# Expert weights exchanged in half slots of 1 MB, with a wait for each half on both sides, and down products in row order

## The reference, cut to what matters

```python
def hier_moe(h, w_router_group, w_router_expert, w_exp_gate, w_exp_up, w_exp_down):
    ...
    out = jnp.zeros((B * T, D), jnp.float32)
    for grp in range(N_GROUPS):
        wgt = comb * (g_sel == grp)[:, None]
        hg = jnp.einsum('nd,edf->enf', hf, w_exp_gate[grp])
        hu = jnp.einsum('nd,edf->enf', hf, w_exp_up[grp])
        hid = jax.nn.silu(hg) * hu * wgt.T[:, :, None]
        out = out + jnp.einsum('enf,efd->nd', hid, w_exp_down[grp])
    return out.reshape(B, T, D)
```

## Time and profile before

| | |
|---|---|
| median of the runs | 1875.35 us (1875.28 to 1878.07, 3 runs) |
| the profiled execution, its own time | 1873.54 us |
| its span, first to last instruction | 1871.8 us |
| mean granted clock of PE | 0.972 of full speed |
| PE busy | 1751.0 us, 94% |
| bytes read from memory | 618.65 MB, 336 GB/s over the span |
| expert loads | 64 of gate, 64 of up, 64 of down, 2048 KB each |

### The profile page before, as it was taken

How to read it: one execution, slowest core, us unless ns; L and a number is a source line. 1 busy time by engine, 2 the same in 40 slices (tenths; PEclk the granted TensorE clock), 3 DMA queues, 4 the chain that set the end, 5 groups by cost and what they waited for, 6 DMA issues and landing times.

```text
span 1871.8 us, 32911 instructions
## 1 busy us (share of the span) xinstructions
PE 1751.0 (94%) x14031; PEld 1106.9 (59%) x14031; DVE 665.4 (36%) x1444; ACT 470.1 (25%) x778; POOL 211.8 (11%) x295
## 2 busy tenths in 40 slices
PE   5689999999989999899899999999999999999997
PEld 2268779988856666799644444445444454444544
DVE  1145554464673544643322222222221222222224
ACT  3044333344531211344411111111111111111114
POOL 1000000011028880343000000000000000000000
PEclk9889999999999999899999999999999999999998
DMA  9989885585388779341799999999999999999993
GB/s 365 419 285 336 295 326 144 188 263 158 131 313 332 302 307 376 100 162 46 320 420 430 428 429 427 430 427 430 427 430 427 430 427 430 427 430 427 430 427 155
DMA packets 124944, 629.64 MB, mean 336 GB/s; under 512 B 10469, under 2 KB 78493, under 8 KB 83360
## 3 DMA queue, kind: packets, MB, share of 16 engines
q1 hardware_dynamic: 118974, 608.45, 80.9%
q0 software_dynamic: 5120, 17.44, 2.7%
q10 hardware_dynamic: 754, 2.33, 0.3%
HBM read 618.65 MB, written 9.56 MB: 336 GB/s over the span
## 4 chain that ended last, share of the span: by engine, by line
PE 42%; DMA 13%; DVE 1%; issue 1%; SPq 0%; ACT 0%; POOL 0%; DVEq 0%; POOLq 0%; ACTq 0%
PE pb L2681 24%; DMA ring<-in_w_exp_gate 13%; PE pb L2655 4%; PE pb L2661 2%; PE pb L2689 2%; PE pb L2032 2%; PE pb L2033 2%; PE pb L2034 1%; PE pb L2662 1%; PE pb L2570 0%; DVE xt L1830 0%; SPq L502 0%; PE pb L2731 0%; PE pb L2577 0%; PE pb L2728 0%
## 5 line engine op out<-in xcount | busy, mean ns | idle before, releaser
L2681 PE MATMUL pb<-ring,pj 128*64 128x512 f32 x2048 | 460.0, 602 | 23.9 <-DMA ring<-in_w_exp_gate 23.0
L2681 PEld LDWEIGHTS pb<-ring,pj 128*64 128x64 f32 x2048 | 149.2, 138 | 298.8 <-issue 294.7
L2032 PE MATMUL pb<-ht_parts,ring_parts 128*128 128x264 f32 x1056 | 309.5, 293 | 7.3 <-DVE ring_parts L1304 6.2
L2033 PE MATMUL pb<-ring_parts 128*128 128x264 f32 x1056 | 302.1, 286 | 0.0
L2034 PE MATMUL pb<-ring_parts 128*128 128x264 f32 x1056 | 301.8, 286 | 0.0
L2689 PE MATMUL pb<-ring,pj 128*64 128x512 f32 x1024 | 223.3, 594 | 0.0
L2032 PEld LDWEIGHTS pb<-ht_parts,ring_parts 128*128 128x128 f32 x1056 | 202.0, 191 | 24.3 <-issue 16.0
L2033 PEld LDWEIGHTS pb<-ring_parts 128*128 128x128 f32 x1056 | 202.0, 191 | 0.0
L2034 PEld LDWEIGHTS pb<-ring_parts 128*128 128x128 f32 x1056 | 200.9, 190 | 0.0
L1304 DVE TENSOR_TENSOR ring_parts<-ring,ring_parts 128x2048 fp32r<-128x2048 f32 x50 | 114.6, 2292 | 173.9 <-ACT ring_parts L789 173.8
L2689 PEld LDWEIGHTS pb<-ring,pj 128*64 128x64 f32 x1024 | 72.2, 137 | 138.9 <-issue 136.9
(11 more groups left out here) (474 smaller groups left out, 1959.2 us busy)
## 6 DMA issues: line engine op xcount, KB each, us to landing
ring<-in_w_exp_gate SPq DMA_DIRECT2D x64, 2048.0 KB, 15.2
ring<-in_w_exp_up SPq DMA_DIRECT2D x64, 2048.0 KB, 17.2
ring<-in_w_exp_down SPq DMA_DIRECT2D x64, 2048.0 KB, 15.7
ring<-in_w_ada SPq DMA_DIRECT2D x32, 2048.0 KB, 14.8
ring<-in_w_in SPq DMA_DIRECT2D x24, 2048.0 KB, 9.4
pj<-in_w_ada SPq DMA_DIRECT2D x32, 1024.0 KB, 7.8
ring<-in_w_ada_final SPq DMA_DIRECT2D x16, 2048.0 KB, 13.0
ring<-in_w_out SPq DMA_DIRECT2D x8, 2048.0 KB, 8.6
```

The source lines that it names most:

```text
L2032: pe.matmul(out, hi[:, k, :], ht_lo[:, k, :], start=(k == 0), stop=False)
L2033: pe.matmul(out, lo[:, k, :], ht_hi[:, k, :], start=False, stop=False)
L2681: last = pe.matmul(pb[step // 2][SLOT * q:SLOT * q + SLOT, :], xg[:, k, SLOT * q:SLOT * q + SLOT], w[q][:, j, :], start=(k == 0), stop=(k ...
```

## The change

A slot is treated as two halves of 1 MB. `half_slot(s, part)` is a half of its columns, `half_full(s, part)` the semaphore that tells of its landing: `m_full{s}a` or `m_full{s}b`, or, for the first halves of slots 0 to 3, the slot's older semaphore `ring_full{s}` with its count at that point.

SyncE issues four loads of 1 MB for a step instead of two of 2 MB: both experts' first halves, then both experts' second halves. A partition now receives 8 KB by a load. The first halves wait for `m_half`, a new semaphore that PE increments in the middle of each step, the second ones for `m_step` as before.

PE waits for the first halves, does half of the step's products, increments `m_half`, waits for the second halves, does the rest and increments `m_step`. In the down steps a half is one row of hidden values (`c`), so the products now go over all four banks for one row and then over all four for the next. A bank is finished, and announced, in the second half of step 5.

To have room for the new semaphores others are joined: `m_wt` and `m_hp` to `m_turn`, `m_sg`, `m_wte` and `m_ht` to `m_act`, `m_ws` and `m_hid` to `m_dve`, `sv_store` and `sv_in` to `sv_moved`, with the counts adjusted. The instructions on ACT, DVE and GpSimd and their order stay.

```diff
@@ slots
+        def half_slot(s, part):
+            return ring[:, s * RING + part * (RING // 2):s * RING + (part + 1) * (RING // 2)]
+
+        def half_full(s, part):
+
+            if part == 0 and s < MIX_SLOTS:
+                return S(f"ring_full{s}"), out_loads(4 + OUT_SLOTS.index(s))
+            return S(f"m_full{s}{'ab'[part]}"), 0
@@ SyncE
-                for q in range(2):
-                    s = moe_slot(step, q)
-                    if freed is not None:
-                        sp.wait_ge(S("m_step"), freed)
...
-                    sp.dma_start(slot(s).rearrange("p (k f) -> p k f", f=src.shape[2]), src)\
-                        .then_inc(S(f"m_full{s}"), 16)
+                for part in range(2):
+                    for q in range(2):
+                        s = moe_slot(step, q)
+                        if freed is not None:
+                            sp.wait_ge(S(("m_half", "m_step")[part]), freed)
...
+                        w, n = (w_exp_gate, w_exp_up, w_exp_down)[step // 2], 4 if step < 4 else 1
+                        at = (step % 2 * 2 + part) * n
+                        src = w[0].rearrange("g e a b -> (g e) a b")[bass.ds(pair * 2 + q, 1)]
+                        src = src.rearrange("o (p k) f -> p (o k) f", p=P)[:, at:at + n, :]
+                        sp.dma_start(half_slot(s, part).rearrange("p (k f) -> p k f", f=src.shape[2]), src)\
+                            .then_inc(half_full(s, part)[0], 16)
@@ PE
-                for q in range(2):
-                    s = moe_slot(step, q)
-                    pe.wait_ge(S(f"m_full{s}"), (t * 2 + step // 3 + 1) * 16)
...
-                    for n in range(4):
-                        for j in range(2):
-                            c = (step - 4) * 2 + j
-                            for q in range(2):
-                                last = pe.matmul(pb[2 + n][SLOT * q:SLOT * q + SLOT, :], hid_t[:, c, SLOT * q:SLOT * q + SLOT],
-                                                 w[q][:, j, n * BANK:(n + 1) * BANK], start=(c == 0), stop=(c == 3))
-                        if step == 5 and n < 3:
-                            last.then_inc(S("m_yb"), 1)
-                last.then_inc(S("m_step"), 1)
+                for part in range(2):
+                    for q in range(2):
+                        full, before = half_full(moe_slot(step, q), part)
+                        pe.wait_ge(full, (t * 2 + step // 3 + 1) * 16 + before)
+                    w = [half_slot(moe_slot(step, q), part) for q in range(2)]
+                    if step < 4:
+                        for j in range(4):
+                            k = step % 2 * 8 + part * 4 + j
...
+                    else:
+                        c = (step - 4) * 2 + part
+                        for n in range(4):
...
+                            if c == 3 and n < 3:
+                                last.then_inc(S("m_yb"), 1)
+                    last.then_inc(S(("m_half", "m_step")[part]), 1)
```

More of the change, by code:

```diff
@@ L486, in expert_load @@
             def expert_load(pair, step, freed=None):
-                for q in range(2):
-                    s = moe_slot(step, q)
-                    if freed is not None:
-                        sp.wait_ge(S("m_step"), freed)
[L492 to L501, removed]
-                    sp.dma_start(slot(s).rearrange("p (k f) -> p k f", f=src.shape[2]), src)\
-                        .then_inc(S(f"m_full{s}"), 16)
+                for part in range(2):
[3 more added lines that the diff above has]
+                            sp.wait_ge(S(("m_half", "m_step")[part]), freed)
+                        elif s < MIX_SLOTS:
+                            sp.wait_ge(S("out_ps"), 8 + 2 * OUT_SLOTS.index(s) + 2)
+                        else:
+                            sp.wait_ge(S("out_ps"), KD)
+                        w, n = (w_exp_gate, w_exp_up, w_exp_down)[step // 2], 4 if step < 4 else 1
[4 more added lines that the diff above has]
+                            .then_inc(half_full(s, part)[0], 16)
             for step in range(3):
@@ L1181, in moe_act @@
                     act.wait_ge(S("m_step"), t * STEPS + 2)
-                    act.activation(sg, pb[0][:], ACT.Silu).then_inc(S("m_sg"), 1)
-                    act.wait_ge(S("m_wt"), t + 1)
-                    act.copy(pwt[:, 0:NP_], pb[7][:, 0:NP_]).then_inc(S("m_wte"), 1)
+                    act.activation(sg, pb[0][:], ACT.Silu).then_inc(S("m_act"), 1)
+                    act.wait_ge(S("m_turn"), t * 2 + 1)
+                    act.copy(pwt[:, 0:NP_], pb[7][:, 0:NP_]).then_inc(S("m_act"), 1)
                     moe_gather_out(ps * GA + i * 4 + 4, 0)
-                    act.wait_ge(S("m_hp"), t + 1)
-                    act.copy(hid_t, pb[6][:].rearrange("p (c s) -> p c s", s=P)).then_inc(S("m_ht"), 1)
+                    act.wait_ge(S("m_turn"), t * 2 + 2)
+                    act.copy(hid_t, pb[6][:].rearrange("p (c s) -> p c s", s=P)).then_inc(S("m_act"), 1)
                     for n in range(4):
@@ L1856, in moe_dve @@
                         last = dve.tensor_copy(w_slot[r, :], pb[6][r, q:q + 1])
-                    last.then_inc(S("m_ws"), 1)
+                    last.then_inc(S("m_dve"), 1)
                     moe_dispatch(ps * 17 + i + 1, i + 1)
-                    dve.wait_ge(S("m_ws"), t + 1)
-                    dve.wait_ge(S("m_sg"), t + 1)
+                    dve.wait_ge(S("m_dve"), t * 2 + 1)
+                    dve.wait_ge(S("m_act"), t * 3 + 1)
                     dve.wait_ge(S("m_step"), t * STEPS + 4)
                     dve.scalar_tensor_tensor(out=sg, in0=sg, scalar=w_slot, in1=pb[1][:], op0=ALU.mult, op1=ALU.mult)\
-                        .then_inc(S("m_hid"), 1)
+                        .then_inc(S("m_dve"), 1)
                     moe_gather_out(ps * GA + i * 4 + 4, 1)
@@ L2671, in moe_step @@
             def moe_step(t, step):
-                for q in range(2):
-                    s = moe_slot(step, q)
-                    pe.wait_ge(S(f"m_full{s}"), (t * 2 + step // 3 + 1) * 16)
[L2676 to L2679, removed]
-                        for q in range(2):
[L2681 to L2684, removed]
-                    for n in range(4):
-                        for j in range(2):
-                            c = (step - 4) * 2 + j
+                for part in range(2):
[6 more added lines that the diff above has]
+                            k = step % 2 * 8 + part * 4 + j
+                            for q in range(2):
+                                last = pe.matmul(pb[step // 2][SLOT * q:SLOT * q + SLOT, :], xg[:, k, SLOT * q:SLOT * q + SLOT],
+                                                 w[q][:, j * FF:(j + 1) * FF], start=(k == 0), stop=(k == KD - 1))
+                    else:
+                        c = (step - 4) * 2 + part
+                        for n in range(4):
@@ L2731, in moe_pe @@
                         last = pe.transpose(pb[7][:, c * P:(c + 1) * P], disp[:, c, :], ident[:])
[L2732 removed]
+                    last.then_inc(S("m_turn"), 1)
                     moe_step(t, 3)
[L2735 removed]
+                    pe.wait_ge(S("m_act"), t * 3 + 2)
                     pe.wait_ge(S("m_dp"), n + 2)
                     moe_gather(0)
[L2738 removed]
+                    pe.wait_ge(S("m_dve"), t * 2 + 2)
                     for c in range(4):
                         last = pe.transpose(pb[6][:, c * P:(c + 1) * P], sg_in_rows[:, c, :], ident[:])
[L2741 removed]
+                    last.then_inc(S("m_turn"), 1)
                     moe_gather(1)
[L2743 removed]
+                    pe.wait_ge(S("m_act"), t * 3 + 3)
                     pe.wait_ge(S("m_add"), t * KD + KD)
```

15 lines of the change are left out of this document (8 added, 7 removed).

## The result

| | before | after |
|---|---|---|
| median of the runs | 1875.35 us (1870.94 to 1880.11, 7 runs) | 1882.74 us (1878.94 to 1885.22, 7 runs) |
| ratio | | 1.0031, 95% interval 1.0017 to 1.0046 |
| span of the profiled execution | 1871.8 us | 1877.1 us |

The changed kernel is slower by 0.31%, about 6 us; the interval reaches from 3 to 9 us, and the two medians themselves lie 7.4 us apart. The forecast was 1881.3 us, and "slower by over 0.2%" with a chance of 0.60.

A forecast was written before the change was run, and what follows sets the result against it. The full DMA queue was taken as the bound. 6.3 and 4.1 us gained against 14.6 and 2.4 lost, by the stream's count +6.0 us, gave 1879.5 for the profiled execution and 1881.3 us for the median; range 1871.5 to 1889.

The forecast's parts named there:

- The queue sets the pace: Loop over expert pairs: the full DMA queue, 428.5 GB/s, sets 58.73 us a pair; PE's own work is 56.21 us.
- The price of 8 KB packets: Expert weight loads: half slots give 8 KB packets, 0.038 us more per MB on 383 MB, 14.6 us lost.
- p: Time 1 MB (1,048,576 bytes) takes in a full queue: 2.447 us before, forecast 2.485 with 8 KB packets.
- The lower bound: Full queue: 8 KB packets cost nothing extra, p = 2.447 us; as rival "faster" 1867.2 us, chance 0.08.
- the upper one: Full queue: from the time of one packet, 8 KB costs 2.2% more for a byte, p = 2.501 us.
- The small-price rival: Full queue: 8 KB packets only 0.5 to 1.3% dearer, p 2.459 to 2.479, 1871.6 to 1879.1 us; chance 0.32.
- The rival with a cost for each load: Expert loads: each pays something queued 2 MB loads hide; at 0.05 us each, +19 us over no price; chance 0.05.
- The sum: Expert stream: start 896.8 plus 383 x 2.485 gives 1848.6, plus 3.6 of products 1852.2 us, +6.0 against before.
- The tail: End of the loop: PE work behind the last byte falls from 7.7 us to 3.6, 4.1 us gained.
- second way of counting: Whole change: 6.3 and 4.1 us gained, 14.6 and 2.4 lost; said to differ from the sum by 0.8 us.
- The dry queue: Loop start, 915 to 945 us: 6.3 us without data, all to go through the earlier release of first halves.
- The clock risk: PE in the last pair: granted clock falls after some 2.3 us waits, costing up to 1.6 us; within the forecast case.

The follow-up runs named there:

- p4_gateup: Kernel before with gate and up loads of 2 MB in four 4 KB runs per partition, down loads untouched: ratio to before 1.0136, +27.0 us to the last product.
- p8_whole: Kernel before with each 2 MB load in two separate 8 KB runs per partition, whole-slot exchange kept: ratio to before 1.0080, +13.7 us to the last product.
- late_release: Changed kernel with both halves requested only when the whole earlier step is through: ratio to before 1.0037, 961.9 us from burst to last product.
- late_start: Changed kernel with PE waiting for both halves before a step's first product, release still by halves: ratio to before 1.0056, 964.0 us to last product.
- row_order: Kernel before with only the down products reordered, row by row over the four banks: ratio to before 1.0006, 952.7 us to last product.
- mixed: Kernel before with halves only in steps 3 to 5 of the first pair, the second and the last pair: 1869.48 us median, ratio to before 0.9967.
- mixed_start: The mixed kernel with halves at the start alone, last pair exchanged whole: 951.8 us from burst to last product, -1.2 against before, one run.

## Why the prediction was right

*The queue sets the pace.* Right. In all kernels with a 128-partition load the pair's period follows the rate and nothing else: 58.7 us at 429 GB/s, 59.64 at 422, 60.5 at 416 (p4_gateup).

*The price of 8 KB packets.* The step on which the sign hung, and right: p = 2.485 us was taken from a stretch of w_ada loads in the earlier trace rows, and 2.485 is what the expert loads take. The lower bound (no price) and the upper one (from the records' durations, 2.501) both missed it. The records do last 315 ns for an 8 KB packet in the changed kernel too, but their sum is 101.3% of the time of 16 engines, so neighbouring ones overlap by about 4 ns, as the choice assumed. The small-price rival, for which the three cycles of the Trainium skill spoke, fell with p8_whole and p4_gateup: about 9 ns a packet. The rival with a cost for each load fell with p8_whole.

*The sum.* From the burst to the last landing it gave 1848.6 - 893.2 = 955.4 us, measured 955.6 and 955.7; to the last product 959.0, measured 959.4 and 959.5; against before +6.0, measured +6.4 and +6.5. The tail was to be 3.6 us and is 3.8. One slip in the forecast changes nothing in this: its second way of counting (14.6 + 2.4 - 6.3 - 4.1) gives +6.6, so the two ways differ by 0.6 us, not 0.8.

*The parts.* The dry queue: gone, as said. But its worth was put at 6.3 us of the sum, and late_release shows 2.4. These are different comparisons. By the count of the queue from burst to last landing, with 3.6 us of start-up, 7.0 us are without data before (945.4 - 3.6 - 382 x 2.447), 2.7 in late_release and 0.2 in the change (955.6 - 3.6 - 383 x 2.485). So most of the dry time is already gone in late_release, where the first burst is 1 MB longer and the packets smaller, and only the rest hangs on `m_half`; the forecast had counted the 2.4 us of that longer burst as a loss of its own. The tail: 4.1 us forecast, 3.9 measured from the last landing; late_start loses 4.5 in all, 1.7 of them by the clock. Row order at nothing: right, by row_order. Joined semaphores and SyncE's issues at nothing have no run of their own; what the sum leaves over is 0.4 us.

*What was off.* PE waits 3.0 us in a pair where 3.4 were forecast; the full waits start at 1195 us, as forecast, with a short one of 0.4 us at 1140. The clock risk was put on the changed kernel, and it was the other way round: from 1100 to 1800 us its clock is 1.00, before 0.99. PE's clock fell after some waits of 2.2 us and more (in every kernel here with a wait for whole slots), never after the waits of 1.2 to 1.4 us of the change. In the steady part that is worth nothing, since the next wait takes it back; at the very end it is worth 1.7 us, and it cost that in late_start, mixed and mixed_start.

*The median.* 1882.74 against 1881.3. A good part of that agreement is luck: medians of the same kernel before were 1875.35, 1873.75 and 1877.28 us over three sets, a spread as large as half the effect, and the changed kernel's median lies 3.8 us above its profiled execution, the fastest of seven, where the forecast added 1.8. The ratios, 1.0031 and 1.0026, are what to go by; the forecast's was 1.0032, well inside their intervals (1.0017 to 1.0046 and 1.0011 to 1.0042).

## What to carry to other kernels

Where a queue is full, count packets before splitting loads: a release that came earlier bought nothing there (late_release: the same 422 GB/s), and each packet costs its price (about 9 ns here) in every pass. Split only where the profile shows the queue dry (the start of a stream) or an engine working behind the last byte (its end), and keep the long runs in between. To price a packet size that the kernel does not have yet at that place, look for another stretch of the same profile with that size and a full queue, and take its rate, not the mean duration of its packets.

## What the runs showed of the hardware

- Queued loads of 128 partitions: 2.447 us for 1 MB in 16 KB packets, 2.485 in 8 KB, 2.558 in 4 KB (by p4_gateup); about 9 ns for each packet on each of the 16 engines. In 8 KB packets loads of 1 MB and of 2 MB ran at the same rate (295.38 and 295.36 MB in 700 us).
- The same bytes in loads of 64 neighbouring partitions move at 216 GB/s instead of 429, and in loads of 32, alternating between the two halves of the partitions, at 250, with all engines busy. This had not been expected at all. A load for half of the partitions was the most expensive split of all that were tried; why, no run shows.
- PE's granted clock went to the lower of its two levels for a part of the next step after some waits of 2.2 to 3.2 us (step 0 then takes 8.78 us in most cases, instead of 7.09), not after others of the same length, and never after waits of 1.6 us or less in the traces with loads of 128 partitions.
